# One copy and one subtraction per chunk of w_down, instead of two and two, in a two-layer encoder trunk

## What is computed

```python
def swiglu(t, w_gate, w_up, w_down):          # w_gate, w_up: 1024 x 2816, w_down: 2816 x 1024
    return (jax.nn.silu(t @ w_gate) * (t @ w_up)) @ w_down

    out = jnp.zeros((B * S, Dm), dtype=jnp.float32)
    for e in range(N_EXPERTS):                # 8
        ye = swiglu(t, w_gate[e], w_up[e], w_down[e]).astype(jnp.float32)
        out = out + gates[:, e:e + 1] * ye
```

## Time and profile before

| | |
|---|---|
| time, median of 3 runs | 1358.74 us (1357.5 to 1359.35) |
| span of the profiled execution | 1353.7 us (first to last instruction; its time with what lies around the span was not taken apart from the three runs) |
| mean granted clock of TensorE in it | 0.936 of full speed |
| busy share of the span | PE 88%, PEld 72%, DVE 70%, ACT 57%, POOL 1% |
| instructions | 16640 |
| HBM traffic | 341.88 MB read, 253 GB/s over the span |
| the eight experts | about 840 us of the span |

### The profile page before, as it was taken

The page is one execution under the profiler, slowest core; times in us unless marked ns, Lnnn a source line. Parts: engine busy times, 40 slices in busy tenths (PEclk is TensorE's granted clock), DMA queues, the critical chain, the costliest instruction groups (busy, mean ns, idle before and its releaser), DMA issues.

```text
span 1353.7 us, 16640 instructions
## 1 busy us (share of the span) xinstructions
PE 1189.7 (88%) x5504; PEld 977.1 (72%) x5504; DVE 949.2 (70%) x886; ACT 775.8 (57%) x853; POOL 15.0 (1%) x45
## 2 busy tenths in 40 slices
PE   3867899998675759989989999999999998998994
PEld 3766688887675547878877877877877886887883
DVE  4272544444455447887887888887887887887886
ACT  4352444442434327766766776776775776775774
POOL 1000000000000000000000000000000000000000
PEclk9968899999785859999999999999999999999998
DMA  8243365553215317998997998997997997997992
GB/s 278 95 156 132 130 195 184 187 173 94 86 63 170 110 63 269 367 357 290 364 364 248 366 365 279 363 366 246 367 367 262 366 366 258 367 367 262 366 365 75
DMA packets 263825, 343.37 MB, mean 254 GB/s; under 512 B 9040, under 2 KB 236384, under 8 KB 263792
## 3 DMA queue, kind: packets, MB, share of 16 engines
q1 hardware_dynamic: 261648, 335.58, 73.5%
q0 software_dynamic: 1856, 6.33, 1.4%
q10 hardware_dynamic: 288, 1.05, 0.2%
HBM read 341.88 MB, written 1.05 MB: 253 GB/s over the span
## 4 chain that ended last, share of the span: by engine, by line
PE 79%; DVE 9%; ACT 7%; issue 3%; DMA 1%; SPq 0%; DVEq 0%; ACTq 0%
PE ps L733 25%; PE ps L734 24%; PE ps L735 24%; ACT hi_gu L528 2%; ACT hi_d L620 2%; PE ps L874 2%; DMA raw_gu<-in_w_in 1%; DVE lo_gu L1019 1%; PE ps L741 1%; PE ps L836 1%; PE ps L967 1%; DVE rows L1056 1%; DVE xt_lo L1283 1%; DVE xt_lo L1258 1%; ACT gains L664 1%
## 5 line engine op out<-in xcount | busy, mean ns | idle before, releaser
L1019 DVE TENSOR_TENSOR lo_gu<-raw_gu,hi_gu 128x2048 fp32r<-128x2048 f32 (+1 forms) x222 | 501.9, 2265 | 74.2 <-ACT hi_gu L528 74.1
L528 ACT CAST hi_gu<-raw_gu 128x2048 fp32r<-128x2048 f32 (+1 forms) x222 | 419.7, 1896 | 37.4 <-PE ps L735 29.6
L733 PE MATMUL ps<-hi_gu,xt_hi 128*128 128x512 f32 (+1 forms) x976 | 391.9, 402 | 9.7 <-DVE xt_lo L1036 7.1
L734 PE MATMUL ps<-lo_gu,xt_hi 128*128 128x512 f32 (+1 forms) x976 | 382.6, 392 | 0.0
L735 PE MATMUL ps<-hi_gu,xt_lo 128*128 128x512 f32 (+1 forms) x976 | 382.0, 391 | 0.0
L620 ACT CAST hi_d<-raw_d 128x1024 fp32r<-128x1024 f32 x198 | 197.8, 1048 | 234.9 <-PE ps L735 234.9
L1176 DVE TENSOR_TENSOR lo_d<-raw_d,hi_d 128x1024 fp32r<-128x1024 f32 x198 | 233.7, 1222 | 66.5 <-ACT hi_d L620 66.3
L733 PEld LDWEIGHTS ps<-hi_gu,xt_hi 128*128 128x128 f32 x976 | 186.4, 191 | 49.2 <-DVE xt_lo L1036 8.3
L735 PEld LDWEIGHTS ps<-hi_gu,xt_lo 128*128 128x128 f32 x976 | 186.1, 191 | 40.9
L734 PEld LDWEIGHTS ps<-lo_gu,xt_hi 128*128 128x128 f32 x976 | 186.7, 191 | 35.9
L733 PE MATMUL ps<-hi_d,ht_hi 128*128 128x512 f32 x440 | 175.2, 398 | 5.4 <-DVE ht_lo L1182 5.4
(11 more groups left out here) (163 smaller groups left out, 789.2 us busy)
## 6 DMA issues: line engine op xcount, KB each, us to landing
raw_gu<-in_moe_w_gate SPq DMA_DIRECT2D x180, 512.0 KB, 5.3
raw_gu<-in_moe_w_up SPq DMA_DIRECT2D x180, 512.0 KB, 6.5
raw_d<-in_moe_w_down SPq DMA_DIRECT2D x88, 1024.0 KB, 7.1
raw_gu<-in_dense_w_gate SPq DMA_DIRECT2D x22, 512.0 KB, 4.0
raw_gu<-in_dense_w_up SPq DMA_DIRECT2D x22, 512.0 KB, 5.0
raw_d<-in_dense_w_down SPq DMA_DIRECT2D x11, 1024.0 KB, 5.0
raw_gu<-in_w_in SPq DMA_DIRECT2D x16, 512.0 KB, 6.9
raw_gu<-in_w_out SPq DMA_DIRECT2D x16, 512.0 KB, 6.0
```

The lines of the kernel that those rows point to most:

```text
L528: act.copy(hi_gu[at], raw_gu[at]).then_inc(gu_hi_done, 1)
L733: pe.matmul(o, a_hi, b_hi, start=first, stop=False)
L734: pe.matmul(o, a_hi, b_lo, start=False, stop=False)
L1019: dve.tensor_tensor(lo_gu[at], raw_gu[at], hi_gu[at].bitcast(F32), ALU.subtract).then_inc(gu_lo_done, 1)
```

## The change

ACT now makes `hi_d` of a chunk with one copy over both halves (128x2048 instead of twice 128x1024), and DVE makes `lo_d` with one subtraction over both. The semaphores `d_hi_done` and `d_lo_done` now count once per chunk instead of twice; the waits of SP, PE and DVE on them are renumbered. PE waits for `lo_d` once, before the first down product, instead of once per half. Nothing else is changed: the loads, the matmuls and the order of the engines' work are the same. The change makes one line out of two in three places, so that the lines of the changed kernel are 1 or 2 lower from there on (620 is 619, 1176 is 1174, 1182 is 1180).

```diff
@@ SP
             def free_down(chunk):
 
                 if not (isinstance(chunk, int) and chunk < 2):
-                    sp.wait_ge(d_lo_done, chunk * 2 - 2)
+                    sp.wait_ge(d_lo_done, chunk - 1)
@@ ACT, split_d
                     if not (isinstance(chunk, int) and chunk == 0):
                         act.wait_ge(d_used, chunk)
-                    for k in range(2):
-                        act.copy(hi_d[:, k, :], raw_d[:, b, k, :]).then_inc(d_hi_done, 1)
+                    act.copy(hi_d[:], raw_d[:, b, :, :]).then_inc(d_hi_done, 1)
@@ PE
                 def down(c, chunk):
                     pe.wait_ge(ht_lo_done, chunk + 1)
+                    pe.wait_ge(d_lo_done, chunk + 1)
                     for k in range(2):
-                        pe.wait_ge(d_lo_done, chunk * 2 + (k + 1))
                         for t in range(nt):
@@ DVE
                 def split_d(c, chunk):
 
                     b = (d_parity0 + c) % 2
-                    for k in range(2):
-                        dve.wait_ge(d_hi_done, chunk * 2 + (k + 1))
-                        dve.tensor_tensor(lo_d[:, k, :], raw_d[:, b, k, :], hi_d[:, k, :].bitcast(F32), ALU.subtract
-                                          ).then_inc(d_lo_done, 1)
+                    dve.wait_ge(d_hi_done, chunk + 1)
+                    dve.tensor_tensor(lo_d[:], raw_d[:, b, :, :], hi_d[:].bitcast(F32), ALU.subtract
+                                      ).then_inc(d_lo_done, 1)
```

## The result

The changed kernel takes 1361.04 us (median of 20 runs, 1356.08 to 1363.34). The kernel before, run beside it, takes 1355.81 (20 runs, 1350.32 to 1359.85). The ratio is 1.0037, with a 95% interval of 1.0024 to 1.0049: slower by 5.2 us between the medians. The forecast was 1364.2, range 1359.4 to 1367.6, and 5.5 us slower: the time lies in the range and the sign is right. The absolute time was forecast too high, because the three runs of before that were shown had a median 2.9 above that of the twenty.

A forecast was written before the change was run, and what follows sets the result against it. PE was taken to bound the kernel nearly everywhere. Delays of 2.9 + 0.2 + 0.8 = 3.9 us plus 1.6 for the clock gave 5.5, added to the median 1358.74: 1364.2 us, range 1359.4 to 1367.6.

The forecast's parts named there:

- What bounds: Whole kernel: PE sets the time nearly everywhere, with 79% of the chain of waits and 8.56 of 8.56 us busy.
- middle steps at 0: Experts' middle steps: the later subtraction fills idle time, `ht_lo` moves 0.05 us, 0.85 us of slack remains, so no cost.
- `lo_d` 0.78 later, `ht_lo` 4.15 after `hi_d`: Each chunk: the subtraction waits for the whole copy, finishing 0.78 us later; `ht_lo` can start 4.15 us after `hi_d` starts.
- Ends +0.36: Ends of the eight experts: part of the delay reaches PE, the scatter comes 0.36 us later, 2.9 us in all.
- step 1 +0.05: Step 1 of four experts, where a table load makes ACT late: 0.05 us more each, 0.2 us in all.
- one wait per chunk instead of two costs 0 on PE: PE's down products: losing the finer waits costs nothing, since they wait for `ht_lo`, made after both halves of `lo_d`.
- Dense end +0.8: End of the dense network: nothing hides the delay, PE's wait for `ht_lo` grows from 3.75 to 4.5, costing 0.8 us.
- Sum without the clock 3.9: Whole kernel: expert ends 2.9, starts of four experts 0.2 and dense network's end 0.8 make 3.9 us slower.
- The clock +1.6: Intervals between expert scatters: later pauses bring one more PE stretch at 1.2 GHz, 1.6 us; called the weakest term.
- An interval that grows from 105.4 to 105.7 comes nearer to a repetition of the slow case: Scatter-to-scatter intervals: the reason given for counting one slow stretch more than the present four.
- My four slow intervals of seven: Profile before, scatter to scatter: four of seven intervals had a half-clock stretch, priced at 1.56 us each.
- The 5.0 between them lie mostly around the span: Profiled span 1353.7 against median 1358.74: the difference lies outside the span, untouched, so the sum was added to the median.

The follow-up runs named there:

- late_1: Changed kernel plus one unread 512-element DVE subtraction ahead of `lo_d` in the experts' middle steps; 1364.82 us, ratio 1.0038 to the kernel before.
- late_2: Changed kernel plus two unread 512-element DVE subtractions ahead of `lo_d` in the experts' middle steps; 1393.69 us, ratio 1.0261 to the kernel before.
- act_merged: Kernel before with ACT's copy merged into one, DVE still making two subtractions, both after that copy; 1363.45 us, ratio 1.0043.
- tail_late: Kernel before, halves kept, but in each network's last chunk DVE waits for both halves and subtracts once; 1367.11 us, ratio 1.0076.
- the filled pair: Kernel before and changed kernel, each with nine unread PE matmuls in the pause before each expert's scatter; 1348.78 and 1352.34 us.
- the later one: Unmodified changed kernel run again beside the kernel before; 1359.69 against 1357.73 us, ratio 1.0023.
- fill_tail_split: Changed kernel with halves again in each network's last chunk, plus nine unread PE matmuls before each scatter; 1351.63 us, ratio 0.9958 to the kernel before.
- fill_more: Kernel before with unread PE matmuls: nine before each scatter, five before the transposes, 14 at the dense network's end; 1347.74 us, ratio 0.9924.
- tail_split: Changed kernel with copy and subtraction by halves again in the last chunk of each network; 1360.65 us, ratio 1.0014 to the kernel before.

## Why the prediction was right, and where a term was off

- **What bounds, and middle steps at 0: right.** 8.56 before and 8.57 after; late_1 and late_2 show the edge of the slack. Of busy time ACT saved 4.4 and DVE 13.1 us by the page, where 8.9 and 7.9 were forecast: the sum is right, the split is not. On DVE `ht_lo` now starts 0.08 before `lo_d` ends (810.78 against 810.86), an overlap that the forecast did not count in busy time.
- **`lo_d` 0.78 later, `ht_lo` 4.15 after `hi_d`: right**, measured 4.15 and 4.16. act_merged and tail_late show the lost overlap as the cause, by either merge alone. The Trainium skill ("Perfetto Trace Analysis", Optimizing Scalar/DVE Operations) says that where these engines are not saturated but leave others waiting, breaking instructions up may let work finish sooner. This case agrees, by 0.31 us an end; the saving of DVE's and ACT's busy time bought nothing.
- **Ends +0.36, step 1 +0.05: a little too large.** Measured 0.31, and -0.05. Both took 0.14 from the end of `ht_lo` to PE's start. In the rows from which it came a separate waiting instruction in PE's queue waits for `ht_lo`, and the first weight load behind it for `lo_d`. In the changed kernel it is the other way round: the separate instruction waits for `lo_d`, which is done earlier, and the weight load itself for `ht_lo`. PE then starts 0.05 after `ht_lo` ends (811.20 to 811.25), as it did before the change at the dense end (332.68 to 332.74). Table-load step 1 after:

```profile
721.89 1.90 ACT L619 CAST hi_d<-raw_d 128x2048 fp32r<-128x2048 f32 x1
...
726.03 0.42 DVE L1180 TENSOR_TENSOR ht_lo<-ps,ht_hi 128x256 fp32r<-128x256 f32 x1
...
726.50 0.50 PE L732 MATMUL ps<-hi_d,ht_hi 128*128 128x512 f32 x1 [0.36 <-DVE ht_lo L1180]
```

  The first down product is 4.61 after `hi_d`, and 4.66 before. That one wait per chunk instead of two costs 0 on PE was thus wrong by those 0.1 us, in its favour, at the starts of four experts. At the expert ends the price was taken from rows of another kind.
- **Dense end +0.8: right**, 0.79.
- **Sum without the clock 3.9: measured 3.5**, by the spans of the filled pair. It includes 0.43 behind the last scatter, of which I had counted none: 0.13 is `lo_gu` of the next stage that lags, and 0.29 is idle time between two DVE instructions at the very end, for which the traces give no reason.
- **The clock +1.6: the term that was off.** "An interval that grows from 105.4 to 105.7 comes nearer to a repetition of the slow case" had no row behind it. Over all executions whose clock is on record the change adds 0.4 +- 0.6 us of it. Filling the pause gains 8.1 us in the kernel before and 8.4 in the changed one; at 1.56 a stretch that is 5.2 and 5.4 slow ends of eight, and the time at half clock falls by 17 and 18 us, five stretches of 3.4. My four slow intervals of seven were those of one profile, of a kernel that has about five. The sum without the clock, 3.9, was the better forecast of the mean difference, 3.6 to 4.0. That 5.5 stands so near the 5.2 of the first comparison is in part luck: the later one gave 3.2 by the means.
- **"The 5.0 between them lie mostly around the span" (span and median): wrong.** Only 1.8 lie around it. The profiled execution thus took about 1355.5, near the median of the twenty (1355.81), and it was the three runs that were long in a spread of 9 us. The clock explains part of that spread: over the 64 executions time and time at half clock go together with a correlation of 0.61.

## What to carry to other kernels

Two operations on two engines that follow each other in pieces are a pipeline; merging the pieces saves a fixed cost of each and takes away the overlap, here 0.16 us of busy time against 0.78 of delay per chunk. It is free where the engine behind has slack of more than the delay, and is paid where that engine has run out of other work: look at the last chunk of each loop, and keep it in pieces. With that (fill_tail_split) the intervals were those of the kernel before, and no version with merged chunks was shown to be faster than its counterpart in halves. Where a pause brings the clock down, compare the two versions with the pause filled before believing a difference of under 1%, and consider keeping the fill: it was worth more than the change, 0.6% with nine unread matmuls an expert and 0.8% with all of fill_more; the step from 0.6 to 0.8 is not clear of the noise.

## What was not expected of the hardware

- DVE stands for 1.6 or for 3.9 us with nothing waited for at the start of its last part, and which of the two changes with what stands elsewhere in the program: 3.9 in the profiles of tail_split, fill_tail_split and late_1, 1.6 in the others, and back to 1.61 with eight memsets ahead of it all. That is 2.3 us, two thirds of what was being measured. The cause is not shown.
- PE starts 0.05 to 0.06 after `ht_lo` ends where the weight load itself holds that wait (all 13 places of the changed kernel, and the dense end before), and 0.13 to 0.14 after where a separate waiting instruction holds it (the starts of four experts before).
- In tail_late, where the stop for `ht_lo` behind the pause of 1.38 is 0.27 and not 0.18, two of eight ends had a further stretch at half clock. That the longer stop is the reason is not shown.
